# Input projection of a hybrid decoder layer as seven Strassen products

## The chip, the cores and the metric

The kernel runs on one core of one Trainium2 chip. The metric is the device time of one execution in microseconds; smaller is better. TensorE (PE) multiplies, VectorE (DVE), ScalarE (ACT) and GpSimd (POOL) do elementwise work, SyncE (SP) issues the DMAs. Each engine runs its own list of instructions in order and waits on semaphores for the others.

## The reference

```python
hn = (_rmsnorm(x, pre_w) * (1.0 + scale[:, None]) + shift[:, None]).astype(x.dtype)
z = hn @ w_in                       # (2048, 1024) @ (1024, 3072), and 32 decode tokens
xa, ga, q, fr, iv, gb = jnp.split(z, ...)          # six blocks of 512 columns
xc, conv_new = _causal_conv(xa, conv0, conv_w, conv_b)
ha, h_new = _rglru(xc, h0, rg_wa, rg_ba, rg_wx, rg_bx, rg_lam)
ya = ha * jax.nn.silu(ga)
f = lbh + (1.0 - lbh) * jax.nn.sigmoid(frh);  k = (1.0 - lbh) * jax.nn.sigmoid(-frh)
ob, S_new = _hgrn2(qh, logf, k, vh, S0)             # vh is iv
yb = _rmsnorm(ob, onorm_w) * jax.nn.silu(gb)
m = jnp.concatenate([ya, yb], axis=-1) @ w_out
x = x + gate[:, None] * _rmsnorm(m, post_w)
```

One layer is computed for a prompt of 2048 tokens and for 8 sequences of 4 decode tokens. Everything is float32. The statement that matters here is `z = hn @ w_in`; its six column blocks feed two recurrences.

## The kernel before

The prompt is worked in eight **bodies** of 256 tokens (T); body one is written apart, bodies two to seven are a hardware loop, body eight is written apart, and a decode part follows. Ahead of body one a prologue loads and multiplies the adaLN weights and prepares the first input weights.

Float32 precision comes from splitting: a matrix is a high half of 16 bits plus a remainder of 16 bits, and `split3` issues three matmuls per tile of 128 contraction rows (high by high, high by low, low by high). The split weights `wih` and `wil` stay in SBUF for the whole run. They are made once, in the prologue and in body one, from twelve pieces of 256 columns each: a DMA into a staging buffer, `head` on ACT (the high half), `rest` on DVE (the remainder). The tokens of the next body are transposed (`turn_x`), scaled and shifted (`hn_out` on ACT, in PSUM) and split into `hnh` (ACT) and `hnl` (`hn_rest`, DVE) near the end of the body before.

In a body PE projects FR and Q (forget gate, query), then IV and GB (value, gate), then the second halves of FR and Q, then XA and GA (recurrence input and gate) in two halves. `project` keeps a weight tile stationary and moves 256 tokens; `project_rows` keeps 128 tokens stationary and moves 512 columns. Results land in two PSUM banks, `ring[0]` and `ring[1]`, each emptied by one or two ACT instructions (`gate_out`, `q_out`, `xa_out`, `ga_out` and the copies into `vv`, `gbs`). Between these pieces stand sixteen steps of the recurrence (`level` on PE, `take` on DVE, two series of eight) and the output projection of the body before (`out_rows` on PE, `m_out` and `x_out` on DVE, `squares_m` on ACT). The seam between two bodies is long: after the last recurrence matmuls (`unit`) DVE runs `state`, `rows`, `input_scale`, `x_out`, and in the next body `recur`; ACT runs `squares_o`, `decay` and `root`, then `gate_out` of the next body; PE has `project` of FR and then `turn_y`, which needs `rows`. The order on every engine is written out by hand, in `body` of each engine.

SP issues all DMAs in one order. In a loop body of the kernel before that is a residual tile in and out and the next token tile, twice.

## Time and profile before

| | us |
|---|---|
| median of three runs | 1014.89 |
| range of the three | 1014.86 to 1016.26 |
| the profiled execution | 1015.58 |
| its span, first to last instruction | 1013.8 |
| mean granted TensorE clock, as a share of 2.4 GHz | 0.984 |

The profile is one execution. Its page gives busy time for each engine, the chain of work that ended last, and the costliest groups; further views give instructions in order of time, busy time by stretch, and groups by line. A row of the timeline reads: start in us, duration in us, engine, line, operation, what it writes and reads, how many in a row, and in brackets the idle time before it with what ended it. Matmuls are pipelined, so the pace of a series is read from the starts and not from the duration of one.

### The profile page before, as it was taken

To read this page: it belongs to the slowest core of one execution; us is meant where nothing else is said; L and a number is where in the kernel's file an instruction comes from. 1 tells how busy PE (TensorE), PEld (TensorE's weight loads), DVE (VectorE), ACT (ScalarE), POOL (GpSimd) and SP (SyncE) were. 2 spreads that over 40 slices of the span, in tenths; PEclk is the share of its full clock that TensorE was granted. 3 is DMA by queue.
4 is the path that set the end of the run, shared out by engine and by line. 5 is a ranking of instruction groups with operands and counts; after the bars stand their busy time and mean duration, and the time that the engine had idled before them with its cause. 6 is when DMAs were issued, how large, how long until landed. Compare 5 with 4: busy or idle time off the path is not lost.

```text
span 1013.8 us, 20053 instructions
## 1 busy us (share of the span) xinstructions
PE 965.2 (95%) x7447; PEld 710.2 (70%) x7502; DVE 585.0 (58%) x1652; ACT 429.9 (42%) x810; POOL 161.9 (16%) x214
## 2 busy tenths in 40 slices
PE   5799968999999999999999999999999999999987
PEld 2567856579766977587757976697659775887554
DVE  2455786446763666357643775466636763477445
ACT  2535476134732374136513471337413651346321
POOL 4000036111120113011201112011201130111112
PEclk9999988999999999999999999999999999999998
DMA  9985211100110011001100011001101010100413
GB/s 313 324 289 167 84 42 45 60 20 3 42 63 0 21 41 63 0 21 42 52 11 21 0 42 63 0 21 41 63 0 41 0 51 1 43 1 25 118 43 112
DMA packets 46590, 60.62 MB, mean 60 GB/s; under 512 B 2748, under 2 KB 40208, under 8 KB 46524
## 3 DMA queue, kind: packets, MB, share of 16 engines
q1 hardware_dynamic: 46524, 59.86, 17.8%
q8 instruction: 27, 0.44, 0.2%
q14 instruction: 39, 0.32, 0.1%
HBM read 48.90 MB, written 10.95 MB: 59 GB/s over the span
## 4 chain that ended last, share of the span: by engine, by line
PE 88%; DVE 5%; DMA 2%; issue 2%; ACT 2%; SPq 1%; DVEq 0%; ACTq 0%
PE ring L392 66%; PE lev L466 7%; PE aux L509 3%; PE okv L493 1%; PE lev L471 1%; PE okv L495 1%; PE okv L494 1%; PE lev L464 1%; DMA woh<-in_ada_w_dram 1%; DMA work<-in_w_in_dram 1%; PE okv L817 1%; PE aux L443 1%; PE aux L479 1%; PE aux L430 1%; PE okv L430 1%
## 5 line engine op out<-in xcount | busy, mean ns | idle before, releaser
L392 PE MATMUL ring<-hnh,wih 128*128 128x256 bf16 (+1 forms) x1152 | 289.4, 262 | 2.6 <-DVE hnl L1281 2.2
L392 PE MATMUL ring<-hnl,wih 128*128 128x256 f16 (+1 forms) x1152 | 289.6, 262 | 0.0
L392 PE MATMUL ring<-hnh,wil 128*128 128x256 bf16 (+1 forms) x1152 | 289.6, 262 | 0.0
L392 PE MATMUL ring<-woh,work 128*128 128x512 f16 x512 | 162.3, 379 | 1.6
L392 PEld LDWEIGHTS ring<-hnh,wih 128*128 128x128 f16 x1152 | 111.8, 99 | 15.1 <-issue 2.2
L1173 DVE TENSOR_TENSOR qq<-qq,gg 128x256 f32<-128x256 f32 x96 | 42.8, 446 | 133.6 <-PE lev L466 95.8
L392 PEld LDWEIGHTS ring<-hnl,wih 128*128 128x128 f16 x1152 | 109.9, 98 | 12.2
L392 PEld LDWEIGHTS ring<-hnh,wil 128*128 128x128 bf16 x1152 | 110.0, 98 | 11.9
L392 PE MATMUL ring<-wih,hnh 128*128 128x512 f16 (+1 forms) x264 | 101.2, 383 | 4.0 <-ACT kk L857 4.0
L392 PE MATMUL ring<-wih,hnl 128*128 128x512 f16 (+1 forms) x264 | 101.1, 383 | 1.4 <-issue 0.2
L1595 POOL TENSOR_TENSOR kk<-kk,cols 128x256 f32<-128x256 f32 x32 | 29.3, 935 | 410.7 <-ACT kk L857 410.7
L392 PE MATMUL ring<-wil,hnh 128*128 128x512 bf16 (+1 forms) x240 | 91.7, 382 | 0.0
L392 PEld LDWEIGHTS ring<-woh,work 128*128 128x128 bf16 (+1 forms) x512 | 50.2, 98 | 54.7
L466 PEld LDWEIGHTS lev<-qq,kk 128*128 128x128 f32 x640 | 80.9, 192 | 10.0 <-issue 3.8
L392 PE MATMUL ring<-wol,work 128*128 128x512 bf16 x225 | 85.3, 379 | 0.0
L466 PE MATMUL lev<-qq,kk 128*128 128x64 f32 x640 | 80.4, 268 | 3.3 <-DVE kk L1174 3.3
L1181 DVE COPY_PREDICATED am<-lmask,lev 128x256 f32<-128x256 uint8 (+1 forms) x112 | 57.2, 510 | 0.0
L1191 DVE SCALAR_TENSOR_TENSOR st<-st,gg,okv 128x128 f32<-128x128 f32 x64 | 19.4, 345 | 63.5 <-PE okv L495 63.5
L867 ACT ACTIVATE ring<-ring 128x512 f32<-128x512 f32 x32 | 18.6, 582 | 83.9 <-DVE work L1212 83.9
L1615 POOL TENSOR_TENSOR ii<-ii,xc 128x512 f32<-128x512 f32 x16 | 22.4, 1398 | 186.6 <-ACT ii L914 186.5
L392 PEld LDWEIGHTS ring<-wih,hnh 128*128 128x128 bf16 (+1 forms) x264 | 28.2, 107 | 29.6 <-ACT kk L857 4.3
L392 PEld LDWEIGHTS ring<-wih,hnl 128*128 128x128 f16 (+1 forms) x264 | 26.0, 99 | 31.9 <-issue 1.3
(313 smaller groups left out, 1573.5 us busy)
## 6 DMA issues: line engine op xcount, KB each, us to landing
xin<-in_x_prompt_dram SPq DMA_DIRECT2D x16, 512.0 KB, 3.3
work<-in_x_prompt_dram SPq DMA_DIRECT2D x16, 512.0 KB, 4.1
out_dram<-work SPq DMA_DIRECT2D x16, 512.0 KB, 2.6
work<-in_ada_w_dram SPq DMA_DIRECT2D x4, 1024.0 KB, 10.4
woh<-in_ada_w_dram SPq DMA_DIRECT2D x4, 1024.0 KB, 11.8
work<-in_w_in_dram SPq DMA_DIRECT2D x4, 1024.0 KB, 8.5
woh<-in_w_in_dram SPq DMA_DIRECT2D x4, 1024.0 KB, 10.2
wol<-in_w_in_dram SPq DMA_DIRECT2D x4, 1024.0 KB, 9.5
```

Of the source, the lines that this page charges most:

```text
L392: last = mm(out, a(k), b(k), start=start and k == ks[0] and j == 0, stop=stop and k == ks[-1] and j == 2)
L430: last = nc.tensor.transpose(bank[:, (k % 2) * T + P * t:(k % 2) * T + P * t + P], xin[:, t, P * k:P * k + P], ident[:, :])
L443: last = nc.tensor.transpose(aux[j][:, T * h + P * t:T * h + P * t + P], gbs[:, t, P * (2 * j + h):P * (2 * j + h) + P], ident[:, :])
L464: last = mm(lev[i % 2][:, P * hc:P * hc + P], k, q, start=True, stop=True)
L466: last = mm(lev[i % 2][:, P // 2 * hc:P // 2 * hc + P // 2], k, blocks(q, m)[:, :, 1, :], start=True, stop=True)
L509: last = mm(aux[(1 + w + p) % 2][:, T * c:T * c + T], wg[:, w, 2 * p + c, :], xc[:, c, :], start=True, stop=True)
L867: A(ring[j % 2][:, :], ring[j % 2][:, :], ACT.Square, accum_out=essq[:, j:j + 1]).then_inc(esq[j % 2].sem, 1)
L1173: V.tensor_tensor(qo, qo, g[:, :, 0:1].to_broadcast([P, nb, m]), ALU.mult).then_inc(q_upd.sem, 1)
L1181: V.copy_predicated(a[:, :, :, 1, :], msk, x).then_inc(amask.sem, 1)
L1191: V.scalar_tensor_tensor(st[:, hd, :], st[:, hd, :], gg[:, o:o + 1], okv[c][:, 2 * P + P * h:3 * P + P * h], ALU.mult, ALU.add).then_inc(s ...
L1595: G.tensor_tensor(kk[:, cols], kk[:, cols], omlb[:, hd:hd + 1].to_broadcast([P, T]), ALU.mult)\
L1615: G.tensor_tensor(ii[:, :, :], ii[:, :, :], xc[:, :, :], ALU.mult).then_inc(ix_ok.sem, 1)
```

## The change

The input projection is computed by the Strassen-Winograd scheme. The 256 tokens of a body are halved, the 1024 contraction rows are halved, and two blocks of columns are taken as the two column halves: 256 columns of Q with 256 of FR, 512 of GB with 512 of IV, 256 of GA with 256 of XA. Seven products of the halved operands replace eight: `NG = 7`, `HK = 4` contraction tiles each.

- **Weights.** For each of six units `u` (512 source columns) DVE makes four sums of quarter blocks (`weight_sum`), and ACT and DVE split seven operands (`head(u, i)`, `rest(u, i)`, each 128x1024) in place of two pieces of 128x2048. The result is 42 granules of 512 KB. Fourteen (units 0 and 3: Q and FR) stay in SBUF in `wres`. The other 28 (GB/IV and GA/XA) are written to DRAM in body one (`store_product`) and read again in every later body through seven buffers `wstr` (`load_product`), each read waiting until PE has used the granule before it in that buffer. The decode part reads sixteen of them once more.
- **Tokens.** `hn_out` writes float32 into SBUF (`xin`), DVE makes four sums (`hn_sums`), and seven operands are split (`hn_head` on ACT, `hn_rest` on DVE, 128x512 each) where four were.
- **Products.** `product_cols` issues 24 matmuls that move 128 tokens, `product_rows` 24 that move 256 columns. Products 0, 2, 4, 6 of a group accumulate in one bank, 1 and 3 in the other, then 5 afresh in that one. ACT copies the bank to `part` after products 0, 1 and 2; DVE adds bank and `part` after products 3, 4 and 5 and so makes three of the four quarters; the fourth is the bank after product 6.

```diff
+            def product_bank(n, G, i):
+                if i in (2, 3, 4):
+                    pe.wait_ge(part_sb.sem, part_sb.at(n, 3 * G + i - 1))
+                elif i > 4:
+                    pe.wait_ge(quad_ok.sem, quad_ok.at(n, 3 * G + i - 4))
+                return ring[(BANK_X[G] + i) % 2] if i != 5 else ring[1 - BANK_X[G]]
+            def product_cols(n, first, G, i):
+                ...
+                for h in range(2):
+                    last = split3(bank[:, P * h:P * h + P], lambda k: wh[:, k, P * h:P * h + P], ...,
+                                  lambda k: hnh[:, i, k, :], lambda k: hnl[:, i, k, :], range(HK), ...)
 # PE, body
-                project(ring[0], FR, 0, n)
-                project(ring[0], FR, 1).then_inc(fr_ps.sem, 1)
+                cols(FRQ0, 0)
+                if not first:
+                    pe.wait_ge(usq.sem, usq.at(n - 1, 5))
+                cols(FRQ0, 1)
+                cols(FRQ0, 2)
                 if not first:
                     turn_y(n - 1, 0)
                     turn_y(n - 1, 1)
-                project(ring[1], Q_, 0)
-                project(ring[1], Q_, 1).then_inc(q_ps.sem, 1)
+                for i in range(3, NG):
+                    cols(FRQ0, i)
+                pe.wait_ge(quad_ok.sem, quad_ok.at(n, 3 * FRQ0 + 3))
+                product_rows(n, first, 0)
 ...
 # ACT, body
+                copies(n, FRQ0)
                 gate_out(n, 0)
 ...
+            def copies(n, G):
+                for j in range(3):
+                    act.wait_ge(prod.sem, ...)
+                    A(part[:, j, 0:w], ring[(BANK_X[G] + j) % 2][:, 0:w], ACT.Copy).then_inc(part_sb.sem, 1)
 # DVE, body
+                add_frq(n, 0, 0)
+                add_frq(n, 0, 1)
                 if not first:
                     recur(n - 1, 1)
+                add_frq(n, 0, 2)
+                if first:
+                    weights_a(1, 2)
 ...
                 recur(n, 0)
                 if not last_body:
                     hn_rest(n + 1, 0)
+                    hn_rest(n + 1, 1)
+                    hn_sums(n + 1)
                 take(n, 1, 7)
+                    for j in range(3, NG):
+                        hn_rest(n + 1, j)
                 conv(n, 1)
```

Three places in the order of the engines follow.

**ACT at the seam** between two bodies: the end of body seven (`aa`, `rr` are `decay` and `root`) and the start of body eight. Before:

```order
L920 ACT_TABLE_LOAD
L920 ACTIVATE aa<-rr,cols 128x256 x2
L922 ACTIVATE rr<-rr,cols 128x256 x2
L926 ACT_TABLE_LOAD
L926 ACTIVATE rr<-rr 128x512
L1061 REGISTER_ALU
L1061 COMPARE_AND_BRANCH
L856 ACT_TABLE_LOAD
L856 ACTIVATE ff<-ring0 128x512
L857 ACTIVATE kk<-ring0 128x512
```

Now:

```order
L1055 ACTIVATE aa<-rr,cols 128x256 x2
L1057 ACTIVATE rr<-rr,cols 128x256 x2
L1061 ACT_TABLE_LOAD
L1061 ACTIVATE rr<-rr 128x512
L1222 REGISTER_ALU
L1222 COMPARE_AND_BRANCH
L981 ACTIVATE part<-ring0 128x256
L981 ACTIVATE part<-ring1 128x256
L981 ACTIVATE part<-ring0 128x256
L991 ACT_TABLE_LOAD
L991 ACTIVATE ff<-kk 128x512
L992 ACTIVATE kk<-kk 128x512
```

Three copies out of the product banks now stand behind `root`, and the gates read `kk` in SBUF, which DVE's add has written.

**ACT in the middle of a loop body**, where the squares of the next tokens (`junk<-xin`) are taken. Now:

```order
L1036 ACTIVATE junk,stat<-xin 128x512
L980 REGISTER_ALU
L981 ACTIVATE part<-ring0 128x256
L980 REGISTER_ALU
L981 ACTIVATE part<-ring1 128x256
L980 REGISTER_ALU
L981 ACTIVATE part<-ring0 128x256
L990 REGISTER_ALU
L991 ACT_TABLE_LOAD
L991 ACTIVATE ff<-kk 128x512
```

Before, the squares were followed by the gates alone, out of `ring0`; now PE's third product of the group waits for the first of these copies.

**DVE in the last quarter of a loop body**, from the end of `recur` to the second convolution (`xc<-xa`). Before:

```order
L1281 TENSOR_TENSOR hnl<-aux1,hnh 128x512
L1153 REGISTER_ALU
L1168 REGISTER_ALU
L1173 TENSOR_TENSOR qq<-qq,gg 128x4x64
L1174 TENSOR_TENSOR kk<-kk,gg 128x4x64
L1176 TENSOR_TENSOR gg<-gg 128x4
L1181 COPY_PREDICATED am<-lmask,lev1 64x4x64
L1239 TENSOR_SCALAR xc<-xa,par 128x256 x2
```

Now:

```order
L1481 TENSOR_TENSOR xin<-xin 128x4x128
L1482 REGISTER_ALU
L1483 TENSOR_TENSOR xin<-xin 128x4x128
L1473 REGISTER_ALU
L1474 TENSOR_TENSOR hnl<-xin,hnh 128x512
L1485 REGISTER_ALU
L1487 TENSOR_TENSOR xin<-xin 128x4x128
L1343 REGISTER_ALU
L1359 REGISTER_ALU
L1364 TENSOR_TENSOR qq<-qq,gg 128x4x64
L1365 TENSOR_TENSOR kk<-kk,gg 128x4x64
```

Where one remainder stood ahead of the last `take`, there are now three remainders and four sums, and four remainders (before, none) stand between that `take` and the convolution; the three that stood behind the convolution are gone from there.

## Rows read from the trace of the kernel before

**Rows 1.** Page, part 1: busy us, share of span, instructions.

```profile
PE 965.2 (95%) x7447; PEld 710.2 (70%) x7502; DVE 585.0 (58%) x1652; ACT 429.9 (42%) x810; POOL 161.9 (16%) x214
```

**Rows 2.** By stretch: length, busy of PE, PEld, DVE, ACT, POOL, clock, DMA share, GB/s.

```profile
0.00:49.00 49.00, 30.77 (x204) 18.07 (x205) 16.06 (x50) 18.97 (x33) 12.03 (x49) 0.97 1.04 318
49.00:158.20 109.20, 96.81 (x788) 76.43 (x792) 76.78 (x140) 61.64 (x86) 18.74 (x18) 0.95 0.46 147
158.20:273.40 115.20, 110.65 (x811) 81.28 (x816) 64.70 (x171) 48.50 (x93) 22.50 (x21) 0.97 0.09 31
...
707.20:815.60 108.40, 108.03 (x811) 80.75 (x816) 63.26 (x184) 46.63 (x92) 15.10 (x19) 1.00 0.07 25
815.60:923.40 107.80, 107.43 (x813) 80.12 (x818) 62.16 (x186) 39.32 (x76) 16.14 (x19) 1.00 0.06 22
923.40:1013.80 90.40, 79.14 (x796) 50.49 (x796) 49.17 (x185) 28.11 (x71) 17.07 (x12) 0.93 0.27 83
```

**Rows 3.** Chain of work that ended last, in order of time: start, us, what.

```profile
63.97 2.59 PE ring L392 x12
...
217.11 15.72 PE ring L392 x144
```

**Rows 4.** Timeline of PE, decode projection: its first matmul and what follows its last.

```profile
923.36 0.18 PE L392 MATMUL ring<-hnh,wih 128*128 128x32 bf16 x1
...
933.13 1.07 PE L443 MATMUL aux<-ident,gbs 128*128 128x128 f32 x8
```

**Rows 5.** Timeline of PE: second half of body seven starts, body eight starts.

```profile
759.11 0.27 PE L392 MATMUL ring<-hnh,wih 128*128 128x256 bf16 x1
...
815.61 0.27 PE L392 MATMUL ring<-hnh,wih 128*128 128x256 bf16 x1
```

**Rows 6.** Timeline of ACT, from the middle of body seven to its end.

```profile
760.03 0.28 ACT L878 ACTIVATE junk<-okv 128x128 bf16<-128x128 f32 x1 [0.59 <-DVE st L1191]
...
763.49 0.19 ACT L901 ACTIVATION_READ_ACCUMULATOR junk<-xin 128x1 f32 x1
...
799.90 0.99 ACT L934 ACTIVATE aux<-aux,shf,sc 128x256 f32<-128x256 f32 x2
...
805.47 0.60 ACT L937 ACTIVATE hnh<-okv 128x512 bf16<-128x512 f32 x1
...
821.94 0.63 ACT L926 ACTIVATE rr<-rr 128x512 f32<-128x512 f32 x1 [0.31 <-DVE rr L1249]
```

**Rows 7.** Timeline of DVE, the same stretch and the start of body eight.

```profile
766.96 1.28 DVE L1226 SCALAR_TENSOR_TENSOR work<-work,stat 128x1024 f32<-128x1024 f32 x1
...
805.12 2.71 DVE L1241 SCALAR_TENSOR_TENSOR xc<-xa,par,xc 128x256 f32<-128x256 f32 x6
...
824.51 1.28 DVE L1226 SCALAR_TENSOR_TENSOR work<-work,stat 128x1024 f32<-128x1024 f32 x1
825.72 1.10 DVE L1254 TENSOR_TENSOR ii<-rr,ii 128x512 f32<-128x512 f32 x1
...
828.51 0.70 DVE L1263 TENSOR_TENSOR sil<-xc,sil 128x512 f32<-128x512 f32 x1
829.68 0.43 DVE L1148 TENSOR_SCALAR ff<-ff 128x512 f32<-128x512 f32 x1 [0.47 <-POOL ff L1599]
```

**Rows 8.** Groups by line: busy us, mean ns of one, idle before.

```profile
L1174 DVE TENSOR_TENSOR kk<-kk,gg 128x256 f32<-128x256 f32 x12 | 5.0, 419 | 0.0
...
L1281 DVE TENSOR_TENSOR hnl<-aux,hnh 128x512 f16<-128x512 f32 x2 | 1.4, 683 | 0.0
```

**Rows 9.** Groups by line, prologue and body one: weight remainder (DVE), high half (ACT).

```profile
L1288 DVE TENSOR_TENSOR wil<-woh,wih 128x2048 bf16<-128x2048 f32 x4 | 9.1, 2286 | 1.1 <-ACT wih L957 1.1
...
L957 ACT ACTIVATE wih<-woh 128x2048 f16<-128x2048 f32 x4 | 7.5, 1902 | 0.0
```

**Rows 10.** Page, part 6: issues, size of one, median us from issue to landing.

```profile
xin<-in_x_prompt_dram SPq DMA_DIRECT2D x16, 512.0 KB, 3.3
```

**Rows 11.** Groups by line, decode projection: weight loads of TensorE.

```profile
L392 PEld LDWEIGHTS ring<-hnh,wih 128*128 128x128 f16 x120 | 9.1, 96 | 0.0
```

More of the change, by code:

```diff
@@ L58 @@
 C_RGLRU = 8.0
+NG = 7
+HK = KT // 2
+NSTR = 4 * NG
 LEVELS = 7
@@ L204, in build @@
         early_ld = [sem(f"early_ld{i}") for i in range(len(early))]
+        w_ld = [Signal(f"w_ld{i}", 16 * NSTR // NG) for i in range(NG)]
         fin = sem("fin")
@@ new lines, in product_rows @@
+            def product_rows(n, first, i):
+                bank = product_bank(n, IVGB, i)
+                for u in (1, 2):
+                    product_ready(n, first, u, i)
+                    wh, wl = granule(u, i)
+                    o = 256 * (u - 1)
+                    split3(bank[:, o:o + 256], lambda k: hnh[:, i, k, :], lambda k: hnl[:, i, k, :],
+                           lambda k: wh[:, k, :], lambda k: wl[:, k, :], range(HK), u == 1 and i in (0, 1, 5), u == 2,
+                           i in (2, 3, 4, 6))                        .then_inc(prod.sem, 1)
@@ L992, in body @@
                 squares_o(n, 1)
-                weights("wi", 7)
+                if first:
+                    for i in range(NG):
+                        head(3, i)
                 if not last_body:
@@ L1011, in body @@
                     last.then_inc(gp_sb, 1)
-                xa_out(n, 0)
-                weights("wi", 11)
+                    for i in range(NG):
+                        head(4, i)
+                copies(n, XAGA0)
                 ga_out(n, 0)
+                if first:
+                    for i in range(NG):
+                        head(5, i)
+                copies(n, XAGA1)
                 gates_out(n, 0)
-                weights("wo", 0)
-                xa_out(n, 1)
                 decay(n, 0)
@@ L1020, in body @@
                 ga_out(n, 1)
+                if first:
+                    out_head(0)
                 if not last_body:
-                    for j in range(4):
-                        hn_out(n + 1, j)
-                weights("wo", 1)
+                    hn_out(n + 1)
+                    hn_head(n + 1)
+                if first:
+                    out_head(1)
                 k_out(n, 1)
@@ L1051, in _ @@
             mod_out(2, lev[0])
[L1052 removed]
             mod_out(3, lev[1])
[L1054 removed]
+            for i in range(NG):
+                head(0, i)
             act.wait_ge(mod_ok, 1)
[L1056 to L1058 removed]
+            hn_out(0)
+            hn_head(0)
             body(0, True, False)
@@ L1327, in body @@
                     y_split(n - 1)
-                for l in range(LEVELS + 1):
+                for l in range(3):
                     take(n, 0, l)
-                    if l == 0:
-                        weights(5)
-                weights(6)
+                    if first:
+                        rest(1, 3 + l)
+                        rest(2, 3 + l)
+                if first:
+                    weight_sum(1, 3)
+                    weight_sum(2, 3)
+                add_ivgb(n, 0)
+                take(n, 0, 3)
+                if first:
+                    rest(1, 6)
+                    rest(2, 6)
+                add_ivgb(n, 1)
+                take(n, 0, 4)
+                add_ivgb(n, 2)
+                for l in range(5, LEVELS + 1):
+                    take(n, 0, l)
                 if not first:
@@ L1347, in body @@
                     x_out(n - 1, 0)
+                for j in range(3):
+                    add_frq(n, 1, j)
+                if first:
+                    weights_a(4)
+                    weights_b(4)
                 forget(n, 1)
-                weights(9, 10)
                 take(n, 1, 0)
+                add_xaga(n, 0, 0)
+                take(n, 1, 1)
+                add_xaga(n, 0, 1)
+                add_xaga(n, 0, 2)
+                if first:
+                    weights_a(5)
+                    weights_b(5)
                 conv(n, 0)
-                weights(11)
-                take(n, 1, 1)
                 take(n, 1, 2)
+                take(n, 1, 3)
                 if first:
```

581 lines of the change are left out of this document (371 added, 210 removed).

## The prediction, made blind

> **What bounds the kernel now.** I read the busy times first [rows 1]: PE is busy 95% of the span, DVE 58%, ACT 42%. Then the busy time by stretch [rows 2]: in a steady body (108.4 us) PE is busy 108.0, DVE 63.3, ACT 46.6. PE never waits there, and nothing but less work on PE can shorten it. The prologue (49.0), body one (109.2) and the decode part (90.4) are mixed; in body one DVE is already busy 76.8 us. So I ask two things: how much PE work goes, and whether the engines that now feed and empty the products keep PE supplied.
>
> **What the products save on PE.** A matmul's cost is its pace. In the chain, 12 matmuls of 512 columns take 2.59 us (216 ns each) and 144 of 256 take 15.72 us (109.2 ns) [rows 3], a line of 0.42 ns a column; 128 columns come to 55.6 ns. That is an extrapolation, and the nearest row bounds it from below: in the decode projection 384 matmuls of 32 columns, each with its own weight load, run from 923.36 to 933.13 us, 25.4 ns each [rows 4]. A weight load fits into 25 ns, so it hides behind 53 ns of moving. From above the row is a load's own record of 96 ns [rows 11]; I take 55.6, since the decode row shows loads back to back. In a body, 384 matmuls of 256 (41.9 us) become 672 of 128 (37.4), and 96 of 512 (20.8) become 168 of 256 (18.3): 7.0 us less, 6.5% of a body.
>
> Against this stands a rule of the Trainium skill, "TensorE: Matmul & The Clock Gate", section Back-to-back issue gap: a stream of load and matmul pairs runs at about 81 ns a matmul for 128 columns. By it the 672 would take 54.4 us, and the projection of a body would be 10.0 us dearer on PE than now, not 7.0 cheaper. The decode row of 25.4 ns a pair speaks against it.
>
> **What a steady body adds elsewhere.** DVE: 12 adds of 256 columns at 0.42 and 3 of 512 at 0.68, three more remainders and four token sums at 0.68 each [rows 8]: 12 us, so 75 us busy. ACT: 12 copies of 256 columns at 0.40, which lies between 0.28 for 128 columns and 0.60 for 512 [rows 6], three of 512, three more high halves, less four evacuations: about 7 us. Neither engine becomes the bound. But the new work stands in series with PE: product 2 waits for the copy of product 0, product 5 for an add, product 6 for another, and only two banks exist. A product lasts 1.33 us, so whichever engine is inside a longer stretch when its copy or add is due stops PE. I went through the body for that.
>
> *First half (from the first product of FR/Q, time 0 at 815.61 [rows 5]).* Products 0 and 1 end at 2.7. Product 2 needs ACT's first copy, which stands behind `root`; `root` ends at 822.57, that is 7.0 [rows 6], held by DVE's `rows` and `input_scale`, which the change leaves alone. With the copy, 7.5: PE waits 4.8. Five products and `turn_y` (1.0, [rows 4]) then end at 15.2. DVE is done with `x_out` at 10.2, adds twice as products 3 and 4 end (13.3), then runs `recur`, 3.5 us in this trace (825.72 to 829.21) [rows 7], and only then the third add: 17.0. PE waits 1.8. IV/GB starts at 17.0 where it started at 11.4 (48 + 48 matmuls of 109.2 ns and `turn_y`). It is 2.4 shorter than before, and one level waits 0.5, since the forget gate goes through ACT and POOL later than before (DVE takes it up at 829.68 now, 14.1 [rows 7]). Half one was 51.9 (108.4 less the 56.5 of half two); plus 5.6, minus 2.4, plus 0.5: 55.6.
>
> *Second half (time 0 at 759.11 [rows 5], 56.5 us long).* The first copy stands behind the squares of the next tokens, which end at 763.68, 4.6 [rows 6]; product 2 could start at 2.7 and starts at 5.1. The first add stands behind `x_out`, which ends at 768.24, 9.1 [rows 7]: 0.5 more. Later DVE puts `conv` (3.4 us) ahead of a `take` that PE needs: 1.2. The last quarter is worst. `hn_out` started at 799.90, 40.8 [rows 6]; with one more add ahead and `ga_out` in two pieces I put it at 41.9, and its eight pieces take 4.0, the first two high halves 1.0 (46.9). In the old order DVE was through the second `conv` at 807.83, 48.7 [rows 7]. Now it runs two remainders, three sums, a remainder and a sum (0.6 each, 50.7), a `take` (1.3), four remainders (2.4) and the `conv` (3.4): 57.6. PE, with three groups shortened by 1.1 each, would be at `gates` at 48.7. So `gates` starts at 57.7, and behind it stand 4.4 us of `gates` and `unit`: 62.1 in place of 56.5. PE's waits in this half sum to about 9 us.
>
> A steady body: 55.6 + 62.1 = 117.7; I take 117.5 (108.4 before). About 16 us of waits take the place of 7 us of work.
>
> **What body one and the prologue add.** A remainder of 2048 columns takes 2.29 us on DVE and a high half 1.90 on ACT [rows 9]; halves of them come to 1.15 and 0.95 from start to start. A unit is 11 DVE operations, 12.7 us, where two pieces took 4.5. In the prologue the first unit stands between the landing of the second piece and the token scaling, in a chain ACT, DVE, ACT, and then come the four token sums: first product at about 62.5 instead of 49.0. In body one DVE gets five units (63) in place of nine pieces (20), and the 12 us above: 132 us busy from 76.8. It waited 32 us and that does not vanish, since `take` needs `level` and the reverse; each unit adds two handshakes of about 1 us with ACT, and DVE's folding of `w_out` waits for a load that SP issues only behind 14 stores of granules (some 6). I take 180 us, between 145 (DVE fully busy but for a tenth) and 200.
>
> **Stores and loads.** 28 granules of 512 KB a body are 14.7 MB in 117 us, 125 GB/s, where the prologue moved 318 GB/s [rows 2]. In IV/GB PE uses two granules in 3.46 us, and a 512 KB load lands in 3.3 us from issue [rows 10]; at 318 GB/s one takes 1.65. Seven buffers are three and a half products of lead. I cost the stream at nothing behind PE's work; were that cover gone it would be the rival below.
>
> **Body two, body eight, decode.** Body two was 6.8 longer than a steady one [rows 2], held by the last pieces of `w_out`, and that stays: 124.3. Body eight has no token split: 113. The decode part has 480 matmuls of 32 columns for 384 (2.4 us more), 120 of 256 for 48 of 512 (2.7 more) and sixteen granules to fetch, nine of them behind their buffers: 97. PE waits of several us were followed by half clock in this trace (body one 0.95, body two 0.97 [rows 2]); I add 5.
>
> **The sum.** 62.5 + 180 + 124.3 + 5 x 117.5 + 113 + 97 + 5 = 1169 us against a span of 1013.8. The execution lay 1.8 above its span and the median 0.7 below the execution, so the time is about **1170 us**. Its own range is 1115 to 1220, set by body one (-35, +20) and by 3 us a body.
>
> **The rivals.**
> - *Only ACT's two places hurt*: the waits behind `root` and behind the squares stay, but DVE catches up elsewhere. A steady body is then about 109.5, 8 us less seven times: 1113. For it: DVE is idle 45 us of a body. Against: its idle time is not where the adds are due.
> - *Every wait is hidden, faster*: a steady body of 101.4 (seven times -7) and a body one in which DVE's waits absorb most new work (+23 with the prologue 13.5): 1014 - 49 + 36 = 1001. It decides at `root`: only if it ended before 2.7 in a body would PE not wait, and it ended at 7.0 in the row.
> - *Weight loads are not hidden at 128 columns*: at 96 ns a pair [rows 11], 27 us of PE work more a body, some 6 of which fall into waits: 1170 + 7 x 21 = 1317. By the Trainium skill's 81 ns (the section above) it is 17 us more, 11 net of waits, 1247; its chance is within this one.
> - *The stream is late*: if a granule took 2.5 us in place of 1.65, IV/GB would need 35 us for 14 against 24 of PE work: 11 a body, 1245.
>
> **How the numbers follow.** My forecast 0.74, ACT's two places alone 0.10, weight loads 0.05, late stream 0.05, every wait hidden 0.04, an exact balance of the two 0.02. The range takes in the milder rival and half of the late stream: 1095 to 1235. A measurement of this kernel can tell about 0.2%. Faster by more than that 0.05, within it 0.02, slower 0.93.
>
> **What would show it.** In the new timeline a product of FR/Q: 24 matmuls in 1.33 us confirm the pace. At each seam PE should idle near 5 us ahead of the third product with ACT's copy as the releaser, about 2.5 us at the same place of the second half, and 3 us ahead of `gates` with DVE's `conv`. The loads should never be the releaser. Body one should be long with DVE busy over 120 us. It is wrong if the steady bodies are under 105 us, or if PE is busy without a break but longer.

## The result

The changed kernel takes **1225.7 us** (median of 4 runs, 1225.3 to 1227.0) where the kernel before takes 1015.4 in the same comparison (4 runs, 1014.9 to 1016.3): ratio 1.208, 95% interval 1.206 to 1.209. It is slower, as forecast, and inside the stated range of 1095 to 1235, but 56 us above its centre of 1170 and 6 us above the range of 1115 to 1220 that the forecast gave to its own mechanism. The profiled execution has a span of 1225.2 us.

The page of the changed kernel: busy times, granted clock in 40 slices, the chain by engine, the instruction queue of part 3 (packets of 16 KB, MB, share) and the stream's loads. The first line answers to [rows 1].

```profile
PE 984.7 (80%) x10519; PEld 822.4 (67%) x10550; DVE 718.9 (59%) x1884; ACT 491.9 (40%) x968; POOL 150.0 (12%) x214
PEclk9988777769999999999999999999899998999897
q8 instruction: 92, 1.51, 0.5%
PE 57%; DVE 22%; issue 8%; ACT 7%; SPq 2%; DMA 2%; DVEq 1%; ACTq 0%
wstr<-w_products SPq DMA_DIRECT2D x212, 512.0 KB, 4.7
```

PE is busy 80% of the span instead of 95%, while DVE (59% for 58%) and ACT (40% for 42%) are about as busy in share as before. No other engine has become the bound: the chain of work that ended last goes back and forth between PE, DVE and ACT. That is a kernel that waits for hand-overs.

By stretch (columns as in [rows 2]; the cuts are the first matmul of body one, two, three, four, five and six; the last row is body eight with the decode part):

```profile
63.02:263.17 200.15, 117.89 (x1169) 105.47 (x1169) 133.96 (x217) 87.09 (x133) 17.73 (x18) 0.75 0.41 149
263.17:396.27 133.10, 108.82 (x1175) 92.32 (x1176) 76.71 (x199) 55.24 (x113) 21.64 (x21) 0.94 0.41 138
396.27:519.38 123.11, 108.67 (x1172) 92.07 (x1177) 74.27 (x209) 52.35 (x108) 13.56 (x19) 0.96 0.43 147
519.38:642.04 122.66, 108.66 (x1173) 92.09 (x1177) 73.84 (x206) 51.91 (x108) 13.56 (x19) 0.96 0.43 147
642.04:761.60 119.56, 105.52 (x1173) 89.19 (x1177) 73.41 (x204) 51.40 (x108) 13.56 (x19) 0.99 0.45 151
1004.70:1225.20 220.50, 190.80 (x2136) 150.91 (x2142) 117.33 (x388) 70.47 (x157) 30.84 (x31) 0.94 0.41 134
```

| stage | forecast | measured | miss |
|---|---|---|---|
| prologue | 62.5 | 63.0 | +0.5 |
| body one | 180 | 200.2 | +20.2 |
| body two | 124.3 | 133.1 | +8.8 |
| bodies three to seven | 587.5 (117.5 each) | 608.4 (121.7 each) | +20.9 |
| body eight | 113 | 117.2 | +4.2 |
| decode part | 97 | 103.2 | +6.2 |
| clock, as a lump | 5 | in the stages | -5 |
| span | 1169.3 | 1225.2 | +55.9 |

Who kept PE waiting in one steady body, by the view of waits (PE alone, 648 to 768 us; columns: waiting group, releaser, us in total, times, longest):

```profile
PE aux L626 <- DVE xc L1432: 3.0, 1, 3.0
PE ring L487 <- ACT part L981: 2.7, 2, 2.0
PE ring L487 <- issue: 2.1, 1, 2.1
PE ring L487 <- DVE qq L1317: 1.6, 1, 1.6
PE aux L596 <- DVE kk L1365: 1.3, 1, 1.3
PE okv L610 <- DVE st L1382: 1.2, 1, 1.2
PE lev L583 <- DVE kk L1365: 1.2, 1, 1.2
PE ring L487 <- ACT sil L1026: 0.7, 1, 0.7
PE ring L487 <- DVE kk L1317: 0.4, 1, 0.4
```

Five of the nine are waits that the forecast named: `gates` behind `conv` (3.0), the third product behind ACT's copy (2.7, of which 2.05 in the second half), the third add behind `recur` (1.6), a level (1.2), the add behind `x_out` (0.4). No load is among them. (The view counts a wait from the modelled end of the matmul before; from start to start each is 0.2 to 0.4 longer.) Four are in no sentence of it: `turn_k` (1.3), `out_rows` behind `ga_out` (0.7), and two that need a look, the one called "issue" and the unit behind `st`. In the kernel before, PE has no wait at all in a steady body by this view. Here the two are in the timeline of the changed kernel, with the `gates` before them:

```profile
631.66 3.20 PE L626 MATMUL aux<-xc,wg 128*128 128x256 f32 x8 [2.97 <-DVE xc L1432]
637.86 0.49 PE L610 MATMUL okv<-vv,am 128*128 128x128 f32 x2 [1.21 <-DVE st L1382]
639.08 0.39 PE L612 MATMUL okv<-vv,ktr 128*128 128x128 f32 x2
642.04 0.23 PE L487 MATMUL ring<-hnh,wres 128*128 128x128 bf16 x1 [2.57 <-issue]
646.67 0.23 PE L487 MATMUL ring<-hnh,wres 128*128 128x128 bf16 x1
648.01 0.39 PE L559 MATMUL aux<-ident,gbs 128*128 128x128 f32 x2
```

And, in the kernel before, the first of six matmuls of `out_rows` and the first of the second unit behind them:

```profile
812.98 0.38 PE L392 MATMUL ring<-woh,work 128*128 128x512 f16 x1
...
814.27 0.38 PE L493 MATMUL okv<-vv,am 128*128 128x128 f32 x2
```

The reader sees three things. First, the eight matmuls of `gates` last 3.2 us here behind their wait; one body later in the same trace they take 1.99. Second, the last `unit` waits for DVE's state step; before, the six matmuls of `out_rows` stood between the two units. Third, between the last unit and the first product of the next body PE stands idle 2.57 us, and the releaser is "issue": it waits for nothing that the profile shows. The third product starts at 646.67 and is over at 648.01, 1.34 us for 24 matmuls.

So one sign that the prediction had named for the seam did not come as told. It wanted near 5 us of idle PE ahead of the third product, behind ACT's copy. At the five seams where PE's loop jumps that wait is 0 to 0.6 us, and 2.1 to 2.6 us of "issue" stand ahead of the first product instead; only at the seam into body eight, which no jump crosses, is it there as forecast (4.4 us).

### The profile page after: what moved, and what is told of

The parts are those of the page before. It is cut to its first block, busy times and chain, and to the rows that moved or that the text cites. A ratio compares the mean times of both kernels' runs of the same rounds, so it can differ in the third digit from the quotient of the medians.

```text
span 1225.2 us, 27701 instructions
## 1 busy us (share of the span) xinstructions
PE 984.7 (80%) x10519; PEld 822.4 (67%) x10550; DVE 718.9 (59%) x1884; ACT 491.9 (40%) x968; POOL 150.0 (12%) x214
## 4 chain that ended last, share of the span: by engine, by line
PE 57%; DVE 22%; issue 8%; ACT 7%; SPq 2%; DMA 2%; DVEq 1%; ACTq 0%
PE ring L487 39%; PE lev L583 5%; PE aux L626 3%; DVE xc L1432 3%; ACT xin L1069 2%; DVE hnl L1474 2%; DVE wstr L1500 2%; PE okv L610 1%; DVE wres L1500 1%; PE okv L612 1%; PE okv L611 1%; SPq L388 1%; DVE xc L1430 1%; DVE rr L1438 1%; PE lev L581 1%
## 5 line engine op out<-in xcount | busy, mean ns | idle before, releaser
L487 PE MATMUL ring<-hnh,wres 128*128 128x128 bf16 (+1 forms) x1952 | 191.6, 233 | 82.1 <-ACT part L981 37.1
L487 PEld LDWEIGHTS ring<-hnh,wres 128*128 128x128 f16 (+1 forms) x1952 | 163.9, 107 | 87.5 <-issue 57.3
L487 PE MATMUL ring<-hnh,wstr 128*128 128x128 bf16 (+1 forms) x1952 | 172.3, 219 | 19.7 <-DVE wstr L1500 8.2
L487 PE MATMUL ring<-hnl,wres 128*128 128x128 f16 (+1 forms) x976 | 184.7, 233 | 0.0
L487 PE MATMUL ring<-wstr,hnh 128*128 128x256 f16 (+3 forms) x944 | 163.9, 279 | 21.5 <-DVE qq L1317 10.6
L487 PEld LDWEIGHTS ring<-hnh,wstr 128*128 128x128 f16 (+1 forms) x1952 | 152.7, 101 | 20.6 <-issue 9.3
L487 PE MATMUL ring<-hnl,wstr 128*128 128x128 f16 (+1 forms) x976 | 165.2, 219 | 0.0
L487 PE MATMUL ring<-wstr,hnl 128*128 128x256 f16 (+1 forms) x472 | 131.6, 279 | 0.0
L487 PEld LDWEIGHTS ring<-hnl,wres 128*128 128x128 f16 x976 | 102.9, 107 | 0.2
L487 PEld LDWEIGHTS ring<-hnl,wstr 128*128 128x128 f16 x976 | 95.9, 100 | 0.1
```

Of the source, the lines that this page charges most:

```text
L487: last = mm(out, a(k), b(k), start=start and k == ks[0] and j == 0, stop=stop and k == ks[-1] and j == 2, skip_group_check=more)
```

## The experiments

The theory: (a) the pace of 128-column matmuls is as forecast; (b) the rest is order, ACT's and DVE's; (c) body one is weight work on DVE; (d) the stream is free. Its rivals: weight loads that do not hide, ACT's two places alone, the stream. Then came "issue" and the half clock, which the first four runs made a question of its own. All ratios are against the kernel before, timed on the same chip.

| run | us | ratio, 95% interval |
|---|---|---|
| changed kernel | 1225.7 | 1.206 to 1.209 |
| p1_pace_128 | 1041.7 | 1.024 to 1.028 |
| p2_pace_unrolled | 1026.3 | 1.009 to 1.013 |
| x1_act_order | 1220.5 | 1.198 to 1.203 |
| x2_conv_first | 1205.4 | 1.184 to 1.188 |
| x3_rows_between | 1226.4 | 1.206 to 1.210 |
| x5_all_unrolled | 1191.4 | 1.171 to 1.176 |
| x6_after_unrolled | 1228.1 | 1.208 to 1.212 |
| x8_order_unrolled | 1193.2 | 1.173 to 1.178 |
| c1_fill | 1215.9 | 1.196 to 1.203 |
| s1_no_stream | 1216.0 | 1.196 to 1.201 |
| w1_slim_weights | 1186.4 | 1.167 to 1.171 |
| w2_pool_memset | 1219.4 | 1.199 to 1.203 |

### The pace, and the loop's jump

```diff
 def project(bank, col, c, n=None):          # in the kernel before
-    for j in range(KT // 2):
-        last = split3(bank[:, T * c:T * c + T], ..., lambda k: hnh[:, k, :], ...)
+    for t in range(NT):
+        to = P * t
+        for j in range(KT // 2):
+            last = split3(bank[:, T * c + to:T * c + to + P], ..., lambda k: hnh[:, k, to:to + P], ...)
```

> The kernel before, with one edit: each 128x128 weight tile of the column products (FR, Q, XA, GA) moves 128 tokens and then the other 128, in two passes, so 384 matmuls of 256 columns a body become 768 of 128, each with its own weight load. Nothing else changes: same waits, same engines, no stream. My theory (weight loads hide, 55.6 ns a matmul): 384 x (2 x 55.6 - 109.2) = 0.8 us more a body, some 6 in all, 1021 us; 24 such matmuls in 1.33 us. Rival (weight loads are not hidden at 128 columns, 81 to 96 ns a pair): 384 x (162 - 109.2) = 20 us a body or more, at least 1170 us.

Measured 1041.7: between the two, and as neither told. The pace itself is the theory's. A body without a jump behind it or a drop of the clock, 731.57 to 841.18 in this run's stretches, against 108.4 before [rows 2]:

```profile
731.57:841.18 109.61, 109.61 (x1200) 86.46 (x1201) 62.22 (x180) 45.09 (x86) 14.71 (x19) 1.00 0.07 26
```

That is 1.2 us for 384 more matmuls (0.8 forecast), each with its own weight load. The rival of 20 us a body is out. The other 16 us stand at the seams. PE's timeline of this run at one of them, and the instruction queue of its page:

```profile
389.98 0.39 PE L497 MATMUL okv<-vv,ktr 128*128 128x128 f32 x2
392.34 0.23 PE L392 MATMUL ring<-hnh,wih 128*128 128x128 bf16 x1 [1.97 <-issue]
...
q8 instruction: 91, 1.49, 0.6%
```

The same line of the page of the kernel before:

```profile
q8 instruction: 27, 0.44, 0.2%
```

No wait stands at that seam, and in the kernel before PE crosses it without a gap [rows 5]. The trace gives the time of each fetch on this queue: in the kernel before there is none between 256 and 815 us, that is, while the loop runs; in the pace run there are about eleven a body, two of them at 389.8 and 392.8, at either side of the gap. A steady body has 811 matmuls and 816 weight loads before [rows 2], 1200 and 1201 in the pace run, 1173 and 1177 in the changed kernel. So the smaller loop is kept and the larger is fetched again at each jump. I wrote PE's loop out to test it:

```diff
-            with pe.Fori(1, BODIES - 1) as n:
+            for n in range(1, BODIES - 1):
                 body(n, False, False)
```

> The pace run (the kernel before with 768 matmuls of 128 columns in place of 384 of 256) with PE's loop over the bodies written out, the other engines' loops left. In the pace run PE stood idle 2.25 to 2.7 us at each of the loop's five jumps, waiting for nothing, with a half clock of 3.4 us behind three of them, and its instruction queue fetched 91 blocks of 16 KB where the kernel before fetched 27. My theory (the loop's body no longer stays in PE's instruction store once it has so many matmuls, and the jump waits for a fetch; in straight code the fetch runs ahead): the gaps and the drops go, 11.7 + 5 us, about 1026 us, which is the kernel before plus 1.2 us a body for the pace. Rival (the gap comes of the small matmuls themselves, at the seam): it stays, 1042 us.

Measured 1026.3, as the theory said: the gaps are gone, and so are all three drops of the clock behind them. Every body is 109.6 us. In the pace run a jump of PE's loop thus costs 2.3 to 2.7 us from start to start and, behind three of the five, 3.4 us at half clock. The Trainium skill, "Runtime: NRT & Kernel Launch", section Instruction fetch mechanics, says that PE's instruction store holds 2048 instructions and is filled in blocks of 16 KiB, and that a taken branch whose target lies outside a window of two such blocks makes the engine wait for a fetch. The size of the store agrees with this case: the loop of 1627 matmuls and loads jumps without a gap, those of 2350 and 2401 do not. The window of two blocks, 512 instructions, does not: the loop before is longer than that, and nothing is fetched on this queue while it runs. Where between 1627 and 2350 the limit lies, no run here tried.

### ScalarE's order

```diff
-                copies(n, FRQ0)
+                if first:
+                    copies(n, FRQ0)
                 gate_out(n, 0)
...
+                copies(n, FRQ1)
                 if not last_body:
                     squares_x(n + 1)
...
-                copies(n, FRQ1)
                 gate_out(n, 1)
...
                 decay(n, 1)
+                if not last_body:
+                    copies(n + 1, FRQ0)
                 root(n, 1)
```

> The changed kernel with only ScalarE's order altered: the three copies of the first FR/Q group of the next body stand ahead of root of this body, and those of the second group ahead of the squares of the next tokens. Rival (only ScalarE's two places hurt): the waits of 4.8 and 2.4 us go and PE runs on, 7 us a body, about 1175 us. My theory: VectorE is late at the same places. At the seam the add behind x_out comes at about 10.6 and the third add behind recur at 15.0 instead of 17.0 from the first product: 2 us a body; at the second group product 5 waits for the add behind x_out until 9.5 where it waited before as well: nothing. In body two the 10.8 us wait behind the last pieces of w_out shrinks by some 8. Together 14 + 8 = 22 us, about 1204 us.

Measured 1220.5. The rival (1175) falls, and so does my gain of 2 us a body: bodies three to seven take 120.5 to 123.4 and on the mean 122.4, where the changed kernel has 121.7, and only bodies one and two are shorter, by 4.4 and 3.1, of which body one's is no more than it differs by itself (see the half clock below). The seam in this run (the last unit starts its last matmul at 632.07), first ACT, then DVE:

```profile
637.01 0.38 ACT L981 ACTIVATE part<-ring 128x256 f32<-128x256 f32 x1
...
640.99 1.28 DVE L1420 SCALAR_TENSOR_TENSOR work<-work,stat 128x1024 f32<-128x1024 f32 x1
644.13 0.75 DVE L1320 TENSOR_TENSOR kk<-ring,part 128x256 f32<-128x256 f32 x2 [1.85 <-PE ring L487]
```

The copy is no longer behind `root`, and the adds wait for PE instead of the reverse. But PE has only come to its third product: it lost 2.4 us at the jump and then ran 3.4 us at half clock. What ScalarE's order gives is taken by what had been hidden under it. At the second half the wait went to the add behind `x_out` (2.88 from start to start, in place of 2.27 and 0.66), as the theory had it.

> The changed kernel with only PE's loop over the bodies written out. The gaps of 2.4 to 2.9 us at its five jumps go. My theory: in the changed kernel as it is, root and ScalarE's copy behind it set the start of the third product 7.4 us after the last unit, so the first two products merely start earlier and the third waits about 4.7 us, as it did in body eight, which stands outside the loop: at most the half clock at the seam changes, 1222 to 1226 us. Rival (the jump is on the path): 2.4 us for each of five, 1213 us or less.

This is the other half of the same question, the changed kernel with PE's loop written out and nothing else. Measured 1228.1, 2 us above the theory's 1222 to 1226: the jump is not on the path, and the rival's 1213 falls. The gaps at the jumps are gone, the first product starts 0.11 us behind the last unit, and the third then waits 4.67 us from start to start. PE's waits from 640 to 765 us in this run:

```profile
PE ring L487 <- ACT part L981: 6.5, 2, 4.4
```

The forecast had 4.8 for that wait. In the loop the jump covered half of it and the half clock behind it most of the rest, so each of the two costs hides the other, and neither run that removed one alone could gain in the loop's bodies.

### VectorE's order

```diff
+                conv(n, 1)
                 if not last_body:
                     for j in range(3, NG):
                         hn_rest(n + 1, j)
-                conv(n, 1)
```

> The changed kernel with only VectorE's order altered: the second conv stands ahead of the last four remainders of the next tokens instead of behind them. My theory: the wait of 3.35 us ahead of gates goes, and with it the half clock behind it (gates and unit took 3.0 where 1.75 is full speed): 4.6 us in each of bodies two to seven, 3.4 in body one, about 1195 us. Rival (VectorE is the limit of that stretch whatever its order): the remainders are now late, the next body's products 1 to 4 or the state step wait for them instead, and the time stays within 3 us of 1226.

Measured 1205.4, 20 us less than the changed kernel where I said 31. Bodies three to seven take 119.1 on the mean instead of 121.7: of the 4.6 us, 2.6 are kept. The wait ahead of `gates` fell from 3.0 to 0.6; the rest went back into the seam, where the third product again waits 1.0 to 2.0 us for the copy behind `root` (0 to 0.6 in the changed kernel), and IV/GB starts 17.9 us behind the last unit instead of 16.9. The rival, VectorE as the limit whatever its order, falls.

```diff
 # PE                                            # DVE and ACT in the same way: m_out and
-    out_rows(ring[1], 1, 1, range(4, KT))...     # squares_m of the last piece go back behind
+    out_rows(ring[1], 1, 1, range(4, 6))         # the first state step and its squares
     gates(n, 1)
     unit(n, 1, 0)
+    out_rows(ring[1], 1, 1, range(6, KT))...
     unit(n, 1, 1)
```

> The changed kernel with the last two of eight contraction steps of out_rows (six matmuls of 512 columns, 1.3 us) put back between the two unit calls of the second half, with m_out and squares_m of that bank put back behind the first state step and its squares, as they stood in the kernel before. My theory: the 1.48 us wait of the second unit for VectorE's state step is filled with 1.3 us of work that stood ahead of gates, where PE waited for conv anyway, so gates start no earlier, and each body is 1.3 to 1.5 us shorter: about 1216 us. Rival (ScalarE's root sets the seam and does not move): the wait is moved to the third product of the next body and the time stays at 1226.

Measured 1226.4: nothing. The expectation contradicts itself, and the trace shows where. The wait of the second unit is filled (1.3 us of work for 1.48 of wait), but the unit starts no earlier for that, and neither does `gates`: its wait grew from 3.35 to 4.64 (both from start to start), and from the start of `gates` to the last unit it is 7.5 us as before. Work moved from one wait into another moves the wait. What it does show is that the unit's wait is the price of taking `out_rows` from there, and that this price was paid for `gates` to wait less.

### All orders at once

> The changed kernel with every reordering at once: ScalarE's copies ahead of root and of the squares, VectorE's second conv ahead of the last four remainders, recur behind the third add of FR/Q, out_rows's last two steps between the units, and PE's loop written out. Separately ScalarE's order gave nothing, since the loop's jump (2.4 us) and the half clock behind it stood at the same place. My theory: with the jump gone the seam is 3.5 us shorter, gates starts without a wait (3.35 and half clock 1.25), and what stays in a body is product 5 behind x_out twice (3.0 and 2.9), a level behind conv (1.4), turn_k (1.7) and some half clock: 113.5 us instead of 122.7, about 1160 us in all. Rival (the jump is not a cost of its own): no better than ScalarE's and VectorE's reorderings added, 1200 us.

> The combination of reorderings again (1191 us), with two differences: the first copy of the next body stands ahead of decay and not behind it, since the third product still waited 2.4 us for it there, and the last steps of out_rows stay where the change put them. My theory: the seam is then set by VectorE's x_out, whose add comes at 10.5 from the last unit where the fifth product waited until 12.9: 2.2 us less a body, about 117 a steady body and 1177 us in all; the copies, once ahead of everything, leave the waits of VectorE. Rival (the copy ahead of decay delays root, recur and the third add by as much): 1191 us.

Measured 1191.4 and 1193.2. The reorderings and the straight loop together give 34 us, more than the rival's 25 and half of what the theory said; the second try, for which the theory said 1177 and the rival 1191, gained nothing more. Of the 36 us between the profiled executions of the changed kernel and of the first try, 20 are in bodies one and two. Bodies three to seven gained 2.7 each, no more than VectorE's order gave alone (2.6), so the straight loop and ScalarE's order still gave them nothing. They take 117.7 to 119.5 in the first and 118.6 to 120.3 in the second. PE's waits in one of the first (613 to 733 us):

```profile
PE ring L487 <- DVE kk L1322: 3.5, 2, 2.7
PE ring L487 <- ACT part L983: 2.2, 1, 2.2
PE aux L626 <- DVE xc L1437: 1.8, 1, 1.8
```

and in one of the second (615 to 735 us):

```profile
PE ring L487 <- DVE kk L1322: 6.2, 2, 3.5
PE aux L559 <- DVE gbs L1399: 1.8, 1, 1.8
```

With the copy ahead of `decay` too, ACT is gone from the head of the list and DVE stands there for more than the same amount. DVE at that seam of the second:

```profile
505.95 1.28 DVE L1422 SCALAR_TENSOR_TENSOR work<-work,stat 128x1024 f32<-128x1024 f32 x1
509.04 0.76 DVE L1322 TENSOR_TENSOR kk<-ring,part 128x256 f32<-128x256 f32 x2 [1.80 <-issue]
```

`x_out` ends at 507.2, the product that the add takes has long been there, and DVE stands 1.80 us at "issue". It is the first instruction of DVE's own loop, which was not written out. The same gap, 1.80 to 2.03 us, stands at each of the five seams that this loop's jump crosses. At the seam into body eight, which none crosses, it is missing, and PE's wait for that add is 1.6 us instead of 3.5 to 3.7. The kernel before has it too, where nobody waits for it:

```profile
719.15 0.90 DVE L1254 TENSOR_TENSOR ii<-rr,ii 128x512 f32<-128x512 f32 x1 [1.76 <-issue]
```

So the gap belongs to DVE's jump; what a run with DVE's loop written out would gain wasn't tried. No order that I found makes this kernel faster than the one before.

### The half clock

```diff
+            def fill(count):
+                for _ in range(count):
+                    mm(lev[0][:, :], yh[:, 0, 0:P], woh[:, 0, 0:512], start=True, stop=True)
...
+                    if i == 2 and not first:
+                        fill(9)
                     cols(FRQ1, i)
...
+                if not first:
+                    fill(14)
                 gates(n, 1)
```

> The changed kernel with more work for PE and none less: in bodies two to eight nine matmuls of 512 columns (1.9 us, their result is never read) stand in the wait of 2.27 us ahead of the third product of the second FR/Q group, and fourteen (3.0 us) in the wait of 3.35 us ahead of gates. My theory (the half clock behind a wait is the wait's doing): gates and unit take 1.75 instead of 3.0 and the products behind the first place lose their 3.4 us at half clock, 1.25 + 1.7 us a body, of which the seam's own wait behind root may take back up to a third as it did when conv went first: about 1208 us, between 1205 and 1213. Rival (the clock falls for another reason, or at fixed times): it falls there or elsewhere all the same, 1226 us or, with the added work partly exposed, more.

Measured 1215.9, 10 us less with 5 us more work for PE in each of seven bodies, though less than the 13 to 21 that I gave. The timeline of PE at `gates`, and a steady body by stretch:

```profile
619.92 3.19 PE L670 MATMUL lev<-woh,work 128*128 128x512 f16 x14
623.05 1.99 PE L626 MATMUL aux<-xc,wg 128*128 128x256 f32 x8
...
511.67:631.52 119.85, 110.46 (x1195) 91.36 (x1200) 73.63 (x206) 51.63 (x108) 13.57 (x19) 0.99 0.44 151
```

`gates` takes 1.99 us instead of 3.20, and the body 119.85 at a granted clock of 0.99 instead of 122.66 at 0.96. From body two on, no filled place is followed by half clock in this trace; in the changed kernel each of the two is in five of the six bodies two to seven. Stretches of 3.4 us at half the pace are left at the seams, where nothing was filled in. So the fall to the lower level (1.2 GHz) at these two places is the doing of the idle PE ahead of it. The idle time does not always bring it: the body from 642.04 to 761.60 of the changed kernel, 119.56 long, was spared both, with the same wait ahead of `gates`:

```profile
753.34 1.99 PE L626 MATMUL aux<-xc,wg 128*128 128x256 f32 x8 [2.97 <-DVE xc L1432]
```

Not all of the 10 us is the clock's. By stage the profiled execution is 3.4 us shorter in body one, which the edit does not reach, 10.5 shorter in bodies two to seven, and 2.7 longer in body eight, where the filling stands in places that have little or no wait. Body one differs by that much without any cause in its code: it takes 195.0, 196.8, 199.9 and 200.2 us in four profiled executions (x3, this run, x6, the changed kernel) in which it is the same code.

### The stream

```diff
 def load_product(g, n):
-    sp.wait_ge(prod.sem, prod.at(n, used_at((g - NG) % NSTR)))
-    sp.dma_start(wstr[:, g % NG, :], wscr[g])...
+    pass
 # and the decode part's loads and PE's waits for all of them go
```

> The changed kernel without the loads of granules from DRAM: in bodies two to eight and in the decode part the products read whatever body one left in the seven buffers, so their values are wrong from body two on; the 28 stores stay. My theory: the stream is hidden in every body, and only the decode part, where one load is waited for 5.9 us, gains: about 1219 us. Rival (the stream is late or disturbs PE's and VectorE's reads): 1200 us or less, with steady bodies shorter than 122.7.

Measured 1216.0. A steady body in this run, with DMA at 27 GB/s instead of 147:

```profile
516.01:638.90 122.89, 108.82 (x1176) 92.07 (x1177) 74.14 (x208) 52.20 (x108) 13.54 (x19) 0.96 0.08 27
```

It is as long as with the stream (122.66). Of the 10 us, 7.4 are in the decode part, where the changed kernel waits 5.9 for a granule; 2.3 have gone by at the end of body one, which is within what body one differs by itself, and 0.9 are in bodies three to seven. The theory holds; the decode's wait belongs in the prediction's sum.

### Body one

```diff
-    A(granule(u, i)[0], raw(u, i), ACT.Copy)
+    q = slice(0, 256) if u in (0, 3) else slice(0, 8)
+    A(granule(u, i)[0][:, :, q], raw(u, i)[:, :, q], ACT.Copy)
 # and the sums and remainders alike; GpSimd also zeroes wstr once, over at 27 us, in the prologue
```

> The changed kernel in which the high halves, sums and remainders of the weight units 1, 2, 4 and 5 are made for 8 of 256 columns only, so the projection is wrong; every operation, wait, store and load is still issued, and unit 3 and the prologue's unit stay whole. It takes some 50 us from VectorE and 27 from ScalarE in body one. My theory: that work is what makes body one 200 us long instead of 109, and what is left is unit 3 (12.7 us), the token sums and the hand-overs: body one 135, about 1161 us. Rival (the hand-overs between ScalarE and VectorE, 14 of them a unit, cost more than the work): body one stays above 165, above 1190 us.

Measured 1186.4; body one by stretch:

```profile
63.00:223.60 160.60, 107.47 (x1171) 99.41 (x1172) 88.33 (x217) 64.23 (x133) 19.25 (x18) 0.78 0.52 187
```

It is 160.6 us long, between the theory's 135 and the rival's 165, as the time is between 1161 and 1190. Taking 45.6 us of work from DVE (134.0 to 88.3) and 23 from ACT took 39.6 us from the body: that much of body one is the width of the weight work, nearly one for one. But with DVE at 88 us busy the body is still 28 us longer than body two. There the waits are those of the order: 11.2 us ahead of `turn_k`, 8.8 ahead of `gates`, 10.6 at the seam. Two of these places had caught my eye in the changed kernel's timeline (GpSimd and VectorE):

```profile
247.64 4.27 POOL L1915 TENSOR_TENSOR wol<-work,woh 128x2048 bf16<-128x2048 f32 x1 [7.85 <-ACT woh L1113]
247.91 4.47 DVE L1430 TENSOR_SCALAR xc<-xa,par 128x256 f32<-128x256 f32 x2
...
268.07 4.05 POOL L1915 TENSOR_TENSOR wol<-work,woh 128x2048 bf16<-128x2048 f32 x1
268.24 4.43 DVE L1438 SCALAR_TENSOR_TENSOR rr<-xc,rr 128x512 f32<-128x512 f32 x1
```

Two operations that elsewhere take 0.73 together, and one that takes 0.68, last as long as the subtraction on GpSimd beside them.

```diff
-    G.tensor_tensor(wol[:, :, cols], stage[place["wo", c]], woh[:, :, cols], ALU.subtract)
+    G.memset(wol[:, :, cols], 0.0)
```

> The changed kernel in which GpSimd writes zeros into the remainders of w_out instead of computing them (four subtractions of 2048 columns, 4.05 to 4.27 us each), so the output projection loses its low part. In the trace VectorE's first conv operations took 4.47 us for two beside one of them at 247.6, where two take 0.73, and input_scale 4.43 us for 0.68 beside another at 268.1. My theory (VectorE is held up while GpSimd subtracts, and both places are on PE's path: gates in body one, and root with the copy behind it in body two): 3.7 us at each, about 1218 us. Rival (the stretch comes of something else or is hidden): 1226 us.

Measured 1219.4, as the theory said within 1.4 us. The same operations beside the memset:

```profile
245.15 1.80 POOL L1915 MEMSET wol<- 128x2048 bf16 x1 [10.08 <-ACT woh L1113]
245.45 1.97 DVE L1430 TENSOR_SCALAR xc<-xa,par 128x256 f32<-128x256 f32 x2
...
262.59 0.68 DVE L1438 SCALAR_TENSOR_TENSOR rr<-xc,rr 128x512 f32<-128x512 f32 x1
```

The second is back to 0.68; the first still ends no earlier than the (shorter) memset. PE's wait ahead of `gates` went from 9.2 to 6.7 and the one at the seam of body two from 10.8 to 7.8, 2.5 and 3.0 us, and body two is 3.6 us shorter. The rows carry this, not the total, since body one alone differs by up to 5 us. The Trainium skill, "SBUF — State Buffer", section SBUF: two separate sides, has the rule: VectorE and GpSimd share one pair of ports, and a VectorE operation in a mode that uses both ports, or one with two inputs in SBUF if the GpSimd operation reads SBUF, is blocked for the whole of a GpSimd instruction that started first. `input_scale`, with two inputs beside the subtraction, agrees: it ends 0.55 us behind it; that `conv`'s first step, with one, runs in such a mode is what the rule would need, and the trace doesn't show it.

## Why the prediction was right, and where its sizes were off

*The sign and the mechanism.* Right. Copies and adds stand in series with two banks, and PE waits where ACT or DVE is inside a longer stretch.

*The range.* The time is inside it by luck. The forecast's own terms, 1169 with 20 us more for body one and 3 for each of seven bodies, reach 1210, not the 1220 that it wrote; the measured 1225.7 is inside 1095 to 1235 only because of the room made for a late stream, and the stream was not late.

*The pace* (55.6 ns, extrapolated, against a load's record of 96 ns). Right: 24 matmuls in 1.34 us, 1.2 us for 384 more in the pace run. (The forecast's two rows give 55.8 by its own line, 0.1 us a body.) Both weight-load rivals fall, that of 96 ns and that of 81 ns a pair.

*The steady body's first half.* Right: 54.8 us where I had 55.6 (from 639.4, the end of the last unit, to 694.24, the first product of the second group). IV/GB starts 16.9 us behind the last unit; I said 17.0. Part of this was luck: two costs lay over each other there, the jump that I hadn't seen and the 4.8 us that I had. The rows for this half came from the one seam of the kernel before that no loop's jump crosses [rows 6, 7], so neither PE's jump nor DVE's 1.8 us could be read in them.

*The steady body's second half.* 65.2 to 67.9 where I had 62.1. The failed step is "behind it stand 4.4 us of `gates` and `unit`". It took the 4.4 from rows in which `out_rows` lay between the units, without asking what the second unit waits for once that cover is gone: 1.48 us. `gates` itself came at 59.1 of this half in the spared body where I had 57.7 (the terms that I listed behind 50.7 add up to 57.8, not 57.6), and at 60.1 in the others. And the half clock, which I had put at 5 us in the whole kernel, comes back in most bodies at both waits: 2.7 us a body for the two (67.9 against 65.2).

*Body one*, 200 for 180. DVE's busy time was right (132 forecast, 134 measured), its idle time was not: 66 us where I implied 48. I gave the five units two hand-overs of about 1 us each, 10 us; DVE waits nine times for ACT's high halves, 17 us. The wait for the load of `w_out`, which I had at 6, is 2.0, and the rest is idle time behind PE, above all behind products and units. The hold by GpSimd is in none of my terms; a run shows 2.5 us of it in PE's wait. That run and the slim weights leave the split of the rest argued from the timeline.

*Body two*, 133.1 for 124.3: GpSimd's hold on `input_scale` (3.7) and the last high half of `w_out` (1.9), which stands ahead of the first copy, make the wait 10.8 where I carried 4.8. The first of these is shown (3.0 us of the wait went with it), the second read from the timeline.

*Decode*, 103.2 for 97: the wait for a granule, 5.9 us, which the run without the stream takes away. *The stream in the bodies*: right, nothing.

*The rivals.* "Only ACT's two places" is out (1220 measured, not 1175). "Every wait is hidden" had its point right: it decides at `root`, and `root` was late.

## What to carry to other kernels

A scheme that saves an eighth of a projection's multiplications but puts a copy or an add between each pair of products must find, for every one of them, an engine that is free at that moment; busy shares of 60% and 40% say nothing on that. When a wait is removed, look at what stood hidden under it before the gain is booked, and when work is taken out from between two waits, ask what the second one will now wait for. Count a loop's instructions when matmuls are made smaller.

## What the runs showed of the hardware that I had not expected

- A loop on PE with 1627 matmuls and weight loads jumps without a gap; with 2350 to 2401 each jump takes 2.3 to 2.9 us from start to start, and the instruction queue fetches some eleven blocks of 16 KB a body. Straight code of the same length shows no gap.
- DVE stands 1.8 to 2.0 us at the jump of its own loop, in the kernel before and in the reordered one alike.
- Adding 5 us of matmuls a body into waits of 2.3 and 3.4 us made bodies two to seven 10.5 us shorter together, since the clock didn't fall behind them.
- A GpSimd subtraction of 2048 columns (4.05 to 4.27 us) beside a VectorE operation with two inputs in SBUF stretches it from 0.68 to 4.43 us, and with it the wait of every engine behind it.
